# Seven-product up stage: GpSimd makes the row sums, VectorE the weight sums from the fourth pair on

## What is computed

```python
xp = xp + _rms(_sq_relu_mlp(_rms(xp, gl[2]), mlp_w1[l], mlp_w2[l]), gl[3])

def _sq_relu_mlp(x, w1, w2):
    return jnp.square(jax.nn.relu(x @ w1)) @ w2      # w1 1024 x 4096, w2 4096 x 1024
```

## Time and profile before

| | us |
|---|---|
| runs (3) | 2149.01, 2152.32, 2152.42; median 2152.32 |
| profiled execution | 2149.68 |
| its span | 2147.8 |
| PE busy | 2076.4 (97%) |
| DVE busy | 1172.6 (55%) |
| ACT busy | 876.8 (41%) |
| POOL busy | 264.2 (12%) |

### The profile page before, as it was taken

How to read it: one execution, slowest core, us unless ns; L and a number is a source line. 1 busy time by engine, 2 the same in 40 slices (tenths; PEclk the granted TensorE clock), 3 DMA queues, 4 the chain that set the end, 5 groups by cost and what they waited for, 6 DMA issues and landing times.

```text
span 2147.8 us, 33339 instructions
## 1 busy us (share of the span) xinstructions
PE 2076.4 (97%) x13611; PEld 1867.7 (87%) x13611; DVE 1172.6 (55%) x1712; ACT 876.8 (41%) x1561; POOL 264.2 (12%) x310
## 2 busy tenths in 40 slices
PE   7999999999998899999999999999999999999998
PEld 7999877777778899999888888889999999888886
DVE  5120287566558787887545477653333335444575
ACT  5111397544435444444423255542222234323243
POOL 1000130000153232321000023310000000000011
PEclk9999999999999999999999999999999999999999
DMA  5331311099421777777876443356665657665474
GB/s 177 85 81 42 128 41 34 1 402 345 143 93 60 271 261 244 260 241 288 285 241 212 158 157 99 127 172 221 218 228 206 230 199 255 240 209 174 157 219 138
DMA packets 205971, 394.30 MB, mean 184 GB/s; under 512 B 18749, under 2 KB 100853, under 8 KB 197500
## 3 DMA queue, kind: packets, MB, share of 16 engines
q1 hardware_dynamic: 199628, 387.45, 52.4%
q10 hardware_dynamic: 6192, 4.72, 0.7%
HBM read 273.12 MB, written 119.24 MB: 183 GB/s over the span
## 4 chain that ended last, share of the span: by engine, by line
PE 71%; DVE 3%; issue 2%; POOL 1%; DMA 1%; ACT 1%; SPq 0%; POOLq 0%; DVEq 0%; ACTq 0%
PE ps L1955 27%; PE ps L1916 17%; PE ps L2568 14%; PE ps L3762 4%; PE ps L1973 3%; PE ps L1413 2%; PE ps L3682 1%; PE ps L1925 1%; PE ps L1434 1%; PE ps L1474 1%; PE ps L3655 1%; DMA wo_raw<-attn_w_out 1%; POOL stats L1532 0%; POOL stats L1529 0%; DMA t_b_raw<-scratch_t_ops 0%
## 5 line engine op out<-in xcount | busy, mean ns | idle before, releaser
L1955 PE MATMUL ps<-t_b_hi,t_a_hi 128*128 128x512 f32 x896 | 352.4, 393 | 4.5 <-DVE t_b_lo L1749 2.5
L1955 PE MATMUL ps<-t_b_lo,t_a_hi 128*128 128x512 f32 x896 | 349.2, 390 | 0.0
L1955 PE MATMUL ps<-t_b_hi,t_a_lo 128*128 128x512 f32 x896 | 349.2, 390 | 0.0
L1746 DVE TENSOR_TENSOR t_a_lo<-t_a_raw,t_a_hi 128x1024 fp32r<-128x1024 f32 x112 | 137.1, 1224 | 291.5 <-ACT t_a_hi L1739 155.2
L1955 PEld LDWEIGHTS ps<-t_b_hi,t_a_hi 128*128 128x128 f32 x896 | 168.6, 188 | 44.0 <-issue 6.8
L1955 PEld LDWEIGHTS ps<-t_b_hi,t_a_lo 128*128 128x128 f32 x896 | 168.5, 188 | 35.4
L1955 PEld LDWEIGHTS ps<-t_b_lo,t_a_hi 128*128 128x128 f32 x896 | 168.7, 188 | 34.6
L1529 POOL TENSOR_SCALAR stats<-stats 128x1 f32<-128x1 f32 x63 | 32.6, 517 | 1157.2 <-ACT t_junk_y L1523 985.1
L1916 PE MATMUL ps<-m_xT_hi,t_w_hi 128*128 128x320 f32 (+1 forms) x736 | 162.6, 328 | 0.0
L1916 PE MATMUL ps<-m_xT_hi,t_w_lo 128*128 128x320 f32 (+1 forms) x736 | 162.6, 328 | 0.0
L1916 PE MATMUL ps<-m_xT_lo,t_w_hi 128*128 128x320 f32 (+1 forms) x736 | 162.6, 328 | 0.0
(11 more groups left out here) (345 smaller groups left out, 4429.6 us busy)
## 6 DMA issues: line engine op xcount, KB each, us to landing
t_a_raw<-scratch_s_ops SPq DMA_DIRECT2D x80, 512.0 KB, 3.9
t_b_raw<-scratch_t_ops SPq DMA_DIRECT2D x80, 512.0 KB, 4.8
scratch_t_ops<-u_t SPq DMA_DIRECT2D x16, 1280.0 KB, 5.6
scratch_s_ops<-u_s SPq DMA_DIRECT2D x16, 1280.0 KB, 4.9
scratch_t_ops<-t_t SPq DMA_DIRECT2D x16, 1280.0 KB, 5.5
scratch_s_ops<-t_s SPq DMA_DIRECT2D x16, 1280.0 KB, 4.5
u_w_e<-mlp_w SPq DMA_DIRECT2D x32, 512.0 KB, 6.9
u_w_raw<-mlp_w SPq DMA_DIRECT2D x16, 1024.0 KB, 7.9
```

The costliest lines, as they stand in the source:

```text
L1746: nc.vector.tensor_tensor(sb.a_lo[g % 3][:], sb.a_raw[:, g % 2], sb.a_hi[g % 3][:].bitcast(F32), ALU.subtract).then_inc(self.operand_lo, 1)
L1955: mm = self.nc.tensor.matmul(self.core.ps[:, self.BANK[idx] + tp, :], a[s][:, kk, tp * P:(tp + 1) * P], w[s][:, kk, :], start=(c == 0 and ...
```

## The change

Three things are moved. (1) The five row sums of every pair go from DVE to POOL, in one piece after the weight sums, and no longer in steps of pair i; POOL waits for all four squares of the pair and for the landing of the s and a stores before. (2) The weight sums of pairs 0, 1 and 2 stay on POOL; those of pairs 3 to 15 go to DVE, two after P6 and two after P2 of the pair before. (3) The five t sums of pair i-1 are now made after P1 (three), P2 (one) and P7 (one) of pair i; those of pair 15 all after its P4. The queue of SP is not edited.

```diff
-    S_AFTER = {P6: (0,), P2: (1, 2), P7: (3,), P5: (4,)}
-    S_FIRST = {P7: (0, 1), P5: (2, 3), P4: (4,)}
-    T_AFTER = {P4: (0,), P3: (1, 2)}
-    T_NEXT = (3, 4)
-    T_LAST = {P7: (0,), P5: (1, 2), P4: (3, 4)}
+    W_AFTER = {P6: (0, 1), P2: (2, 3)}
+    T_AFTER = {P1: (0, 1, 2), P2: (3,), P7: (4,)}
...
     def up_pool(self, pool):
-        self.sum_weights(pool, 1)
+        self.sum_weights(pool, self.nc.gpsimd.tensor_tensor, 1)
+        self.sum_weights(pool, self.nc.gpsimd.tensor_tensor, 2)
         for i in range(PAIRS):
-            if i + 2 < PAIRS:
-                self.sum_weights(pool, i + 2)
+            self.combine_s(pool, i)
             self.copy_samples(pool, i)
...
-    def combine_s(self, dve, i, piece):
+    def combine_s(self, pool, i):
...
+        pool.wait_ge(self.squared, 4 * (i + 1) + (i == 0))
+        if i >= 1:
+            pool.wait_ge(self.s_stored[(i - 1) % 2], 32 * ((i - 1) // 2 + 1))
+        add(s[:, 0, :], a11, a12, ALU.add)
+        add(s[:, 1, :], a21, a22, ALU.add)
+        add(s[:, 2, :], a11, a22, ALU.add)
+        add(s[:, 3, :], a21, a11, ALU.subtract)
+        add(s[:, 4, :], a12, a22, ALU.subtract).then_inc(self.s_ready, 1)
...
-        if x == self.P1:
-            return [(i - 1, n) for n in (self.T_NEXT if i > 2 else (1, 2, 3, 4))]
-        after = self.T_LAST if i == PAIRS - 1 else self.T_AFTER
-        return [(i, n) for n in after.get(x, ())]
+        if i == PAIRS - 1 and x == self.P4:
+            return [(i, n) for n in range(5)]
+        return [(i - 1, n) for n in self.T_AFTER.get(x, ()) if (i, n) != (2, 0)]
...
-        for piece in self.s_pieces(i, x):
-            self.combine_s(dve, i - 1, piece)
+        if 2 <= i < PAIRS - 1 and x in self.W_AFTER:
+            self.sum_weights(dve, self.nc.vector.tensor_tensor, i + 1, self.W_AFTER[x])
```

More of the change, by code:

```diff
@@ L2230, in up_loads, with sum_weights @@
         self.store_s(sp, PAIRS - 1)
-    def sum_weights(self, pool, i):
-        s, add = i % 2, self.nc.gpsimd.tensor_tensor
+    def sum_weights(self, eng, add, i, pieces=(0, 1, 2, 3)):
+        s = i % 2
         n = 4 * i
[L2238 to L2241, removed]
+        if 0 in pieces:
+            if i >= 2:
+                eng.wait_ge(self.multiplied, self.done(i - 2, self.P3))
+            self.wait_e0(eng, i)
+            self.wait_e1(eng, i)
         a11, a12 = self.e0[s][:, 0:KT // 2, :], self.e0[s][:, KT // 2:, :]
@@ L2244, in sum_weights @@
         s1, s2, s4 = (self.w_sum[s][:, x] for x in range(3))
[L2245 to L2250, removed]
+        if 0 in pieces:
+            add(s1, a21, a22, ALU.add).then_inc(self.w_summed, 1)
+        if 1 in pieces:
+            eng.wait_ge(self.w_summed, n + 1)
+            add(s2, s1, a11, ALU.subtract).then_inc(self.w_summed, 1)
+        if 2 in pieces:
+            add(a21, a11, a21, ALU.subtract).then_inc(self.w_summed, 1)
+        if 3 in pieces:
+            eng.wait_ge(self.w_summed, n + 2)
+            add(s4, a12, s2, ALU.subtract).then_inc(self.w_summed, 1)
     def copy_samples(self, pool, i):
@@ L2446, in take_out @@
                                      ALU.add).then_inc(self.added, 1)
-    def combine_s(self, dve, i, piece):
-        s = self.one_s
+    def combine_s(self, pool, i):
+        s, add = self.one_s, self.nc.gpsimd.tensor_tensor
         a11, a21, a12, a22 = (self.block(i, b)[:, 0:512] for b in range(4))
[L2452 to L2460, removed]
+        pool.wait_ge(self.squared, 4 * (i + 1) + (i == 0))
[6 more added lines that the diff above has]
+        add(s[:, 4, :], a12, a22, ALU.subtract).then_inc(self.s_ready, 1)
     def combine_t(self, dve, i, piece):
@@ L2474, in combine_t @@
             op.then_inc(self.t_ready, 1)
[L2476 to L2480, removed]
     def t_pieces(self, i, x):
@@ L2533, in dve_up @@
         self.split_operands_lo(dve, 1)
-        for piece in range(5):
-            self.combine_s(dve, PAIRS - 1, piece)
     def wait_place(self, pe, i, x):
@@ L2978, in _ @@
                 if j == 3:
-                    m0.sum_weights(pool, 0)
+                    m0.sum_weights(pool, nc.gpsimd.tensor_tensor, 0)
                 if 3 <= j <= 4:
```

## The result

The changed kernel takes **2247.08 us** (median of 4 runs, 2241.66 to 2249.49) where the kernel before, run beside it, takes 2150.66 (4 runs, 2147.54 to 2152.42): a ratio of 1.0441, 95% interval 1.0426 to 1.0457. The forecast was 2252 with a range of 2185 to 2275. Its profiled execution took 2241.66 us with a span of 2239.9, so the span grew by 92.1 us. It is the fastest of the four, 5.4 us under their median, so what is read from its trace adds up to 92 and not to the 96 us of the medians.

A forecast was written before the change was run, and what follows sets the result against it. PE, busy 97%, was taken to bound the kernel. Pairs growing from 21.05 to 28.3 us gave +95.4 to the last U2, the end +5.0; +100.4 on 2149.7, then 2.6 for the median: 2252 us, range 2185 to 2275.

The forecast's parts named there:

- five marks: Up stage: PE waits before P7 and P4, U2 28 us apart, bunched stores, alternating DMA share, POOL with U2, 1.7 us sums.
- the burst: SP's queue, every pair: six transfers, the t, s and a stores and three loads, leave together once late t is ready.
- A to T: Each up-stage pair, landing of s and a (U2 may start) to t ready: DVE's list with POOL collisions, 11.9 us.
- T to A: Each up-stage pair, t ready to landing of a, which frees U2 of the next pair: 16.4 us, bounds 14.2 to 18.0.
- Start: Pair 0 of the up stage: t ready 2.4 us later, at 701.8, so U2 of pair 2 at 718.2.
- End: From U2 of pair 15 to the down stage: about 22.5 us in place of 17.5, +5.0.
- Sum: Whole kernel: +100.4 us on the profiled 2149.7 gives 2250; median of runs 2.6 above that execution, so 2252.
- PE's clock off the cycle: Up-stage pairs: some 2 us lost to a slower PE clock after waits fit in 7 us of room, adding nothing.
- (a): Rival, up-stage pairs: late burst but no DVE and POOL collisions, 23.7 us a pair, +40, 2192 us; chance 0.07.
- (b): Rival: nothing changes, engine time alone decides and the queue keeps up, 2152 us; chance 0.06.
- (c): Rival, start of up stage: faster, PE's 2.12 and part of its 7.33 us wait go, at most to 2143; chance 0.05.
- (d): Rival, up-stage pairs: only part of the cycle bites, fewer collisions or a faster burst, 2200 to 2222 us; chance 0.10.

The follow-up runs named there:

- e1: Changed kernel with only the t sums put back into the steps of the kernel before: 2157.68 us, ratio 1.0027.
- e2: Kernel before with only the t sums moved to the late steps of the changed kernel: 2236.62 us, ratio 1.0394.
- e3: Changed kernel with s and a of a pair stored ahead of its t in SP's queue, t sums still late: 2176.18 us, ratio 1.0114.
- e4: Changed kernel with four of five POOL row sums left out from pair 1 on: 2194.47 us, ratio 1.0199.
- e6: Changed kernel loading only one of two w2 rows per pair from pair 2 on, 512 KB less: 2226.66 us, ratio 1.0351.
- e5: Kernel before with queue and t reordered (s and a stored ahead of t and next w2), row sums of pair 0 earlier: 2142.46 us, ratio 0.9961.
- e7: Changed kernel, row sums on POOL and weight sums on DVE, with e5's order of queue and t: 2152.08 us, ratio 1.0005.

## Why the prediction was right

**The mechanism was right.** Its five marks are in the trace: the waits before P7 and P4, the burst, POOL starting with U2, the splits and sums at 1.7 us, DMA and DVE in turn. e1 and e2 show that the moved t is what does it, e3 that it works through the queue, e4 and e6 that the two terms are what the forecast called them, a list with collisions and a burst by its bytes.

**A to T: 11.9 forecast, 11.8 measured** in every pair read. Without collisions the forecast had 7.3, and e4, with one POOL sum left, took 7.6. The forecast worked these out by letting the engines go one by one, 0.60 and 1.10 us; the rows show that alternation for five operations in a row. The Trainium skill (Trainium Architecture — The Big Picture, What this means for kernel authors) calls the port pair shared by DVE and GpSimd "an exclusive lock (not a bandwidth split)"; the trace agrees, with the sums of DVE 1.70 us apart beside POOL and 0.60 alone, each POOL sum costing 1.06 in e4.

**T to A: 16.4 forecast, 15.7 on average.** This is the mis-sized term. Thirteen pairs took 1078.17 - 720.30 = 357.9 us, 27.5 each, where the forecast had 28.3 each and 1.5 off, 366.4: 8.5 us too long. The first cycles did take 16.3 and 16.5, the others 15.0 to 16.7: the forecast took the one burst that it could see as the size of all, and its bounds, 14.2 to 18.0, held the rest. Why some bursts are faster was not settled. The traced execution is 5.4 us under the median; if all of that lay in these pairs, the median one would have a T to A of about 16.1, an estimate. So part of the 8.5 us may be the execution and not the term.

**Start.** T of pair 0 was forecast 2.4 us later, U2 of pair 2 at 718.2. They came at 703.99 and 720.30, but the first addition of the stage was at 674.35 in this execution and at 672.06 in that of before, so 2.3 us come from ahead of the stage; without them, 701.7 and 718.0.

**End.** Forecast 22.5 us from the last U2 to the down stage, measured 1099.57 - 1078.17 = 21.4 (before 17.5). T came at 7.0 (forecast 7.1), the w2 rows 8.2 later (forecast the same), as this row of DVE shows:

```profile
1093.36 3.10 DVE L2473 TENSOR_TENSOR u_t<-u_w_raw 128x512 f32<-128x512 f32 x5 [4.30 <-DMA u_w_raw<-mlp_w]
```

**Sum.** In spans: start +4.4 (2.4 forecast), thirteen pairs +84.5 (93.0 forecast), end +3.9 (5.0), rest of the kernel -0.8 (0); together 92.0 where 100.4 was forecast. Between the medians it is 96.4. (Two slips in the forecast's own sums change nothing: its +72 for the fastest burst belongs to 2224, not 2222, and five t sums after 7.1 and 8.2 us end at 18.4, not 18.6.)

**PE's clock off the cycle** held: PE was busy 30 us longer and the granted clock was 0.84 and 0.90 in two of the windows above, but in every pair from 2 to 15 U2 came with the landing of a (POOL's first row sum, let go by that store, starts 0.05 or 0.06 us after it), and a pair took A to T plus T to A and nothing for PE. The waits were smaller for that than the 3 to 4 us that the forecast named: after the two of the start they sum to 55.1 us in 24, 2.3 each and 4.2 a pair, and the slower matmuls are the other 2.2 of the 6.5 us by which a pair grew. Those for U3 are mostly 3.6 us, those for U2 from 0.3 to 3.2, and two pairs have none for U2. That half of the mark, the size, was wrong.

**The rivals.** (a), no collisions, 2192, is nearly e4, which keeps one sum of five: 2194. (b), nothing changes, needed a queue that keeps up with a late t, and it did not; where t is early (e1) the exchange alone comes near it, 2158. (c), faster through the two waits of the earlier trace rows, had the right place for a gain but the wrong edit: e5 gets it, 2142 (the rival's 2143), by the order of the queue and of the first sums, with the row sums left on DVE. (d), a part of the cycle, was not seen.

## What to carry to other kernels

Before moving a step, list what stands behind its store in its queue and which buffers those transfers free; a store that is made late belongs behind the ones that the next iteration waits for, as in e5. When one landing releases two engines that add in SBUF, count their operations as one list: beside PE, in the steady pairs of e1 and e7, the collisions cost nothing, and on the cycle they cost 53 us of the kernel (e4). A change that loses can point to the gain: here the wait at the start of the kernel before was the same cycle, once.

## What the runs showed of the hardware

- DVE's additions out of PSUM keep 0.71 us beside POOL's sums, where two-input operations out of SBUF go from 0.60 to 1.70 us from start to start; in e7 the same collisions cost nothing in the pairs from 3 to 15, and e7 is 5.3 us over e5 at the start of the stage.
- The burst moves 316 to 332 GB/s at a DMA share of 0.92 to 0.96, stores and loads mixed, and a landing late in it comes by the bytes ahead of it, 1.2 us for 0.5 MB by the traces, 1.6 by the medians.
- Not expected: in the 11.8 us with PE's waits of 3.17 and 2.07 us the mean granted clock was 0.84, and 0.90 in the next 15.6, in which PE had no gap. In the following 11.8 us, with waits of 0.82 and 3.58, it was 0.98. It cost nothing here only because PE was not what the pair waited for.
